# Units behind a norm done by halves of the tokens: the first gate unit of the two last FFNs and the first two units of the second gated-delta mixer

## The chip, the cores and the metric

The kernel runs on one core of a Trainium2 chip. The metric is the device time of one execution in microseconds. Three runs of the kernel before took 2135.91, 2136.45 and 2140.04 us, so the median is 2136.45 us.

## The reference

Six layers work on one sequence of 256 tokens with 1024 features, in float32. Layers 0 to 3 are post-norm: a mixer (gated delta net, HGRN2, GLA, gated delta net again), a layer norm over the scaled residual, a SwiGLU FFN of inner width 2816, and a layer norm again. Layers 4 and 5 are pre-norm: an RMS norm, a mixer of four parallel parts, the residual, an RMS norm, and an FFN whose inner activations go through a causal convolution of three taps before the gate.

```python
# layers 0 to 3
x = layer_norm(DN_ALPHA * x + m, mix_ln_g[i], mix_ln_b[i])
x = layer_norm(DN_ALPHA * x + swiglu(x, ffn_w_in[i], ffn_w_down[i]), ffn_ln_g[i], ffn_ln_b[i])
# layers 4 and 5, the FFN
h = rms_norm(x, ffn_norm_g[l])
u = causal_dwconv(jnp.einsum("bsd,df->bsf", h, ffn_w_in[l]), ffn_conv_w[l]) + ffn_conv_b[l]
gate, up = _split(u, (D_FF_2, D_FF_2))
x = x + jnp.einsum("bsf,fd->bsd", jax.nn.silu(gate) * up, ffn_w_out[l])
```

The mixer of layer 3 begins with a projection `x @ w_in` to 4112 columns: queries, keys and values (which go through a causal convolution of four taps), a gate, and 16 columns that hold beta and the decay of the eight heads.

## The kernel before

**Products.** A float32 product is done as three products of type fp32r. Weights and activations are each split into a high part (a cast to fp32r) and a low part (the rest): high times high, low weights times high activations, high weights times low activations. The activations of a stage stand in `xh` and `xl` as 8 tiles of 128 features by 256 tokens.

**Units.** Weights come in units of at most 128 x 2048 elements through a ring of six slots (SyncE starts the loads). ScalarE or VectorE casts a unit to its high part (`w_hi` or `w_extra`, L1624 and L2223), VectorE subtracts for the low part (`w_lo`, L2225; for some units GpSimd does three quarters, L1546). `pe_unit` is ticked when TensorE has done a unit, and that frees its slots.

**Two layouts of the result.** `token_products` (L586) has 128 tokens as the stationary operand and 512 channels as the moving one. `products` (L554) is channel-major: the weights are stationary, 128 channels at a time, and all 256 tokens are moving, so that the causal convolution runs along the free axis. A unit of 256 channels has two column tiles, 8 feature tiles and 3 products, so 48 matmuls, each with its own stationary operand. The first unit of the mixer in layer 3 (`pair8`) has only 40 columns and 24 matmuls.

**Behind a norm.** A norm is done by halves of 128 tokens (t = 0, 1), and each half by two chunks of 512 features (c = 0, 1). VectorE writes the normed rows (L2184), TensorE transposes them, four transposes to a chunk (`rows_to_channels`, L637, into a PSUM bank), ScalarE casts the bank to `xh` (`rows_high`), and VectorE subtracts for `xl` (`low_rows`). In `conv_ffn` (layers 4 and 5) and in `project` for the mixer of layer 3 TensorE does all sixteen transposes before the first matmul, and the matmuls with feature tile k wait for the chunk k // 4 of both halves (`all_rows`).

**Order of the work.** Every engine has its own queue, written out by hand, and runs it in order. In the RMS norm ahead of an FFN of layers 4 and 5 ScalarE does the squares of all four chunks of x first, then the four `rows_high`, then two casts of weights. In the layer norm ahead of layer 3's mixer VectorE does residual and statistics of half 0, its normed rows, residual and statistics of half 1, its normed rows, and then the four `low_rows` together (`all_at_once`); for the other layer norms the two `low_rows` of half 0 stand between the two chunks of half 1.

Of the kernel before, what the change touches and what calls it, by code (L numbers as in the profile page):

```python
# [29 lines left out]
P = 128  # L30
T = 256
D = 1024
KT = D // P
# [9 lines left out]
HALF = 128  # L43
ALL = slice(0, T)
# [173 lines left out]
def build(nc, A, out, book, layers=len(CHAIN)):  # L218

    book.restart()  # L220
    with ExitStack() as ctx:
# [31 lines left out]
        cols = sb("cols", [P, 4, 16])  # L253
# [40 lines left out]
        xh = over("xh", [P, KT, T], "inv")  # L294
        xl = over("xl", [P, KT, T], "xn")
# [226 lines left out]
        def _(pe):  # L522
            unit = fillers = 0

            def products(u, outs, tiles, width, moving, first=True, last=True, i=None, high_ready=None, low_ready=None,
                         part=range(10 ** 6)):


                n = tiles * width
                w_high = high_part(u)[:, 0:n].rearrange("p (k n) -> p k n", k=tiles)  # L530
                w_low = w_lo[:, u % RING, 0:n].rearrange("p (k n) -> p k n", k=tiles)
                x_high, x_low = moving
                if 0 in part:
                    pe.wait_ge(*hi_done(u, i))
                orders = [("high", w_high, x_high), ("w low", w_low, x_high), ("x low", w_high, x_low)]
                if not high_ready:
                    orders[1:] = orders[:0:-1]
                count = 0
                for step, (what, w, xin) in enumerate(orders):
                    if what == "w low" and count in part:  # L540
                        for low_part in lo_done(u, i):
                            pe.wait_ge(*low_part)
                    ready = high_ready if what == "high" else low_ready if what == "x low" else None
                    for j, (cols, c0, cw, tokens) in enumerate(outs):
                        for k in range(tiles):
                            count += 1
                            if count - 1 not in part:
                                continue
                            if ready and j == 0:
                                for what_ready in ready(k):  # L550
                                    pe.wait_ge(*what_ready)
                            wk, xk = w[:, k, c0:c0 + cw], xin[:, k, tokens]

                            m = nc.tensor.matmul(cols, *((wk, xk) if tokens == ALL else (xk, wk)),  # L554
                                                 start=(first and step == 0 and k == 0 and (j % 2 == 0)),
                                                 stop=(last and step == 2 and k == tiles - 1), skip_group_check=True)
                return m
# [93 lines left out]
            def project(layer, kind, norm):  # L651
                nonlocal unit
                psum.next = 4
                for n, (c0, w, how, name, idx) in enumerate(units_in(kind)):
                    if how == "tok0":
                        keys = ("unit", layer, n), ("unit", layer, n + 1)
                        if n == 0:
                            pair = [psum.claim(pe, "proj", layer, n, t) for t in range(2)]
                            second = [psum.claim(pe, "proj", layer, 2, t) for t in range(2)] if kind != "four" else [None]
                            pair_after_norm(unit, pair, norm, keys, second[0])  # L660
                        else:
                            token_pair(unit, second, keys)
                        unit += 2
                        continue
                    if how == "tok1":
                        continue
                    if late_gates(kind) and n >= len(units_in(kind)) - 2:
                        continue
                    ready = {}
                    if n == 0 and layer == 0:  # L670
                        pe.wait_ge(*pool_setup.at("gaps"))
                    if n == 0:
                        for t in range(2):
                            for c in range(2):
                                rows_to_channels(norm, t, c)
                        ready = all_rows(norm)
                    b = psum.claim(pe, "proj", layer, n)
                    left, right = b[:, 0:T], b[:, T:2 * T]
                    outs = {"cm": [(left, 0, P, ALL), (right, P, P, ALL)],
                            "pair8": [(b[0:40, 0:T], 0, 40, ALL)],  # L680
                            "row16": [(b[0:16, 0:T], 0, 16, ALL)],
                            "rest": [(b[0:100, 0:T], 0, 100, ALL)],

                            }[how]
                    products(unit, outs, KT, w, (xh, xl), **ready).then_inc(*pe_unit.tick("unit", layer, n))
                    unit += 1
                    if layer == 0 and n == 2:
                        params_to_columns()
                    if kind == "four":
                        four_ahead(layer, n)  # L690
                    if kind == "gla" and n == 6:
                        gla_gates(layer)
                    if kind == "gdn" and n == 4:
                        if layer == 0:
                            pe.wait_ge(*dve_setup.at("pick"))
                        gdn_columns(layer)
                    if kind == "gdn" and n >= N_CONV + 1:
                        qk_sums(layer, ((0, 1, 2), (3, 4, 5), (6, 7), ())[n - N_CONV - 1])
                    if kind == "gdn" and n == N_CONV + 3:
                        gdn_values(layer)  # L700
                        gdn_spread(layer, 0)
                        gdn_spread(layer, 1)

            def all_rows(norm):
                return {"high_ready": lambda k: (act_norm.at("x hi", norm, 0, k // 4), act_norm.at("x hi", norm, 1, k // 4)),
                        "low_ready": lambda k: (dve_norm.at("x lo", norm, 0, k // 4), dve_norm.at("x lo", norm, 1, k // 4))}
# [146 lines left out]
            def conv_ffn(layer, norm):  # L853

                nonlocal unit

                def gate_up(par_, key, i, freed, parts_ready={}):
                    nonlocal unit
                    for part in range(2):
                        b = banks[4 + 2 * par_ + part]  # L860
                        if freed is not None:
                            pe.wait_ge(*freed[part])
                        products(unit, [(b[:, 0:T], 0, P, ALL), (b[:, T:2 * T], P, P, ALL)], KT, T, (xh, xl), i=i,
                                 **(parts_ready if part == 0 else {}))\
                            .then_inc(*pe_unit.tick("gate" if part == 0 else "up", layer, key))
                        unit += 1

# [3 lines left out]
                def freed_by(k, ago=0):  # L871
                    return dve_ffn.at("conv gate", layer, k, ago=ago), dve_ffn.at("conv up", layer, k, ago=ago)

                for t in range(2):
                    for c in range(2):
                        rows_to_channels(norm, t, c, bank=2 * t + c)
                for b in range(4, 8):
                    psum.claim(pe, "ffn", layer, b, bank=b)
                gate_up(0, 0, None, None, all_rows(norm))
                gate_up(1, 1, None, None)  # L880
                for b in range(4):
                    psum.claim(pe, "ffn", layer, b, bank=b)
# [65 lines left out]
            def gdn_spread(layer, h):  # L948

                b = psum.claim(pe, "bcast", layer, h)  # L950
                for n, part in enumerate((rows_hi, rows_lo)):
                    m = nc.tensor.matmul(b[:, :], pick[0:8, h:h + 1].to_broadcast([8, P]),
                                         part[0:8, :, :].rearrange("p a n -> p (a n)"), start=(n == 0), stop=(n == 1))
                m.then_inc(*pe_gdn.tick("bcast", layer, h))
# [1215 lines left out]
        def _(dve):  # L2170
# [252 lines left out]
            def layer_norm(n, key, next_kind):  # L2423
# [21 lines left out]

                if key[0] == "out":
                    split(2)
                to_rms, all_at_once = next_kind == "four", next_kind == "gdn"
                chunk(0, 0)
                chunk(0, 1)  # L2450
                mean(0)
# [3 lines left out]
                if to_rms:  # L2455
                    dve.wait_ge(*gains_loaded(n + 1))
                    gained_rows(n + 1, 0)
                elif not all_at_once:
                    low_rows(n, 0, 0)
                    low_rows(n, 0, 1)  # L2460
                chunk(1, 1)
# [6 lines left out]
                normed(1, 1)  # L2468
                if to_rms:
                    gained_rows(n + 1, 1)  # L2470
                elif all_at_once:
                    low_rows(n, 0, 0)
                    low_rows(n, 0, 1)
                last = n + 1 if to_rms else n
                low_rows(last, 1, 0)
                low_rows(last, 1, 1)
# [488 lines left out]
```

## Time and profile before

| what | value |
|---|---|
| median of three runs | 2136.45 us |
| the profiled execution, its own time | 2137.8 us |
| its span | 2136.1 us |
| TensorE matmul busy | 2077.8 us, 97% |
| TensorE weight load busy | 1805.2 us, 85% |
| VectorE busy | 1488.5 us, 70% |
| ScalarE busy | 891.5 us, 42% |
| mean share of the granted TensorE clock | 0.993 |

PE is the matmul side of TensorE, PEld its weight loads, which run beside the matmuls. Both are pipelined: the duration of one matmul (283 ns with 256 moving columns) is longer than the distance from its start to the start of the next. So distances are read from a group's first start and the next group's first start, divided by the number of instructions, and not from the mean duration.

### The profile page before, as it was taken

The numbers are of one execution on the slowest core, as the hardware profiler recorded it, in microseconds if no ns is written. First come the engines' busy times: TensorE is split into PE (matmuls) and PEld (weight loads), VectorE is DVE, ScalarE is ACT, GpSimd is POOL, SyncE is SP. The second block draws the span as 40 slices with busy tenths as digits, with TensorE's granted clock in tenths as the row PEclk, the third lists the DMA queues.
The fourth block names the chain that finished last, engine by engine and source line by source line (L and its number), as shares of the span: only waits on it lengthen the run. The fifth ranks groups of instructions, "written<-read, shape, count | busy, mean of one in ns | idle before, by whom it ended". The sixth has DMA issues, their size and how long they took to land.

```text
span 2136.1 us, 35611 instructions
## 1 busy us (share of the span) xinstructions
PE 2077.8 (97%) x14377; PEld 1805.2 (85%) x14377; DVE 1488.5 (70%) x1941; ACT 891.5 (42%) x1174; POOL 177.8 (8%) x152
## 2 busy tenths in 40 slices
PE   7999999999999999999899999999989999999999
PEld 7988888798888798888798878887869998778998
DVE  5957754778854677744696685456688877588887
ACT  2254444334434423444323454445554334663332
POOL 5720000000000000000063300000100000100000
PEclk9999999999999999999999999999999999999999
DMA  7511655553555553555464046554325555414552
GB/s 227 178 61 61 205 189 191 170 190 99 180 196 182 173 178 119 197 192 182 139 180 155 3 149 216 186 186 154 103 78 171 186 183 170 138 50 158 194 180 99
DMA packets 267625, 333.81 MB, mean 156 GB/s; under 512 B 20562, under 2 KB 230613, under 8 KB 267493
## 3 DMA queue, kind: packets, MB, share of 16 engines
q1 hardware_dynamic: 267493, 331.93, 47.8%
q8 instruction: 98, 1.61, 0.3%
q14 instruction: 34, 0.28, 0.0%
HBM read 330.84 MB, written 1.05 MB: 155 GB/s over the span
## 4 chain that ended last, share of the span: by engine, by line
PE 86%; DVE 8%; ACT 3%; issue 2%; SPq 1%; DMA 0%; DVEq 0%; ACTq 0%
PE bank L586 45%; PE bank L554 29%; PE bank L1056 2%; DVE w_lo L2225 1%; ACT stat L1579 1%; PE bank L820 1%; PE bank L637 1%; DVE sq L2184 1%; PE bank L912 1%; PE bank L982 1%; PE bank L1137 1%; DVE pj L2184 1%; PE bank L926 1%; DVE xt L2184 1%; ACT w_hi L1624 1%
## 5 line engine op out<-in xcount | busy, mean ns | idle before, releaser
L2225 DVE TENSOR_TENSOR w_lo<-ring,w_hi 128x2048 fp32r<-128x2048 f32 (+2 forms) x289 | 615.2, 2131 | 375.3 <-ACT w_hi L1624 372.9
L1624 ACT ACTIVATE w_hi<-ring 128x2048 fp32r<-128x2048 f32 (+1 forms) x220 | 418.9, 1905 | 472.6 <-PE bank L586 287.3
L586 PE MATMUL bank<-w_lo,xh 128*128 128x512 f32 x992 | 267.7, 393 | 0.0
L554 PE MATMUL bank<-xh,w_hi 128*128 128x256 f32 x1752 | 239.9, 290 | 5.8 <-DVE w_hi L2223 5.0
L554 PE MATMUL bank<-xh,w_lo 128*128 128x256 f32 (+2 forms) x1832 | 242.4, 285 | 0.0
L586 PE MATMUL bank<-w_hi,xl 128*128 128x512 f32 x896 | 240.6, 390 | 1.0 <-DVE xl L2174 0.9
L586 PE MATMUL bank<-w_hi,xh 128*128 128x512 f32 x896 | 240.9, 391 | 0.6 <-ACT xh L1579 0.6
L554 PEld LDWEIGHTS bank<-xh,w_hi 128*128 128x128 f32 x1752 | 225.0, 195 | 15.8 <-issue 10.2
L554 PEld LDWEIGHTS bank<-xh,w_lo 128*128 128x128 f32 (+2 forms) x1832 | 229.1, 191 | 1.3
L554 PE MATMUL bank<-xl,w_hi 128*128 128x256 f32 x1752 | 230.1, 284 | 0.0
L554 PEld LDWEIGHTS bank<-xl,w_hi 128*128 128x128 f32 x1752 | 219.2, 192 | 0.4
L586 PEld LDWEIGHTS bank<-w_lo,xh 128*128 128x128 f32 x992 | 184.9, 188 | 37.9 <-DVE w_lo L2225 0.6
L586 PEld LDWEIGHTS bank<-w_hi,xh 128*128 128x128 f32 x896 | 167.1, 188 | 37.5 <-issue 2.0
L586 PEld LDWEIGHTS bank<-w_hi,xl 128*128 128x128 f32 x896 | 167.5, 188 | 36.9 <-DVE xl L2174 2.3
L1546 POOL TENSOR_TENSOR w_lo<-ring,w_hi 128x1536 fp32r<-128x1536 f32 x26 | 104.5, 4019 | 959.5 <-DVE w_hi L2223 959.5
L586 PE MATMUL bank<-w_hi,hid_hi 128*128 128x512 f32 x528 | 167.3, 398 | 2.0 <-DVE hid_lo L2174 2.0
L586 PE MATMUL bank<-w_hi,hid_lo 128*128 128x512 f32 x528 | 163.4, 391 | 0.0
L586 PE MATMUL bank<-w_lo,hid_hi 128*128 128x512 f32 x528 | 163.0, 390 | 0.0
L1579 ACT ACTIVATE yb<-bank 128x256 f32<-128x256 f32 (+4 forms) x146 | 58.9, 403 | 164.8 <-PE bank L586 124.9
L586 PEld LDWEIGHTS bank<-w_hi,hid_lo 128*128 128x128 f32 x528 | 99.1, 188 | 21.5
L586 PEld LDWEIGHTS bank<-w_lo,hid_hi 128*128 128x128 f32 x528 | 99.1, 188 | 21.5
L586 PEld LDWEIGHTS bank<-w_hi,hid_hi 128*128 128x128 f32 x528 | 94.6, 189 | 19.5 <-DVE hid_lo L2174 3.7
(323 smaller groups left out, 2406.0 us busy)
## 6 DMA issues: line engine op xcount, KB each, us to landing
ring<-in_ffn_w_in_dram SPq DMA_DIRECT2D x264, 512.0 KB, 4.4
ring<-in_ffn_w_down_dram SPq DMA_DIRECT2D x88, 512.0 KB, 4.1
ring<-in_gdn_w_in_dram SPq DMA_DIRECT2D x64, 512.0 KB, 5.0
ring<-in_ffn_w_out_dram SPq DMA_DIRECT2D x44, 512.0 KB, 3.9
ring<-in_w_in_dram SPq DMA_DIRECT2D x40, 512.0 KB, 4.7
ring<-in_hgrn_w_in_dram SPq DMA_DIRECT2D x32, 512.0 KB, 4.5
ring<-in_gla_w_in_dram SPq DMA_DIRECT2D x24, 512.0 KB, 4.6
ring<-in_gdn_w_out_dram SPq DMA_DIRECT2D x16, 512.0 KB, 4.5
```

The source lines that it names most:

```text
L554: m = nc.tensor.matmul(cols, *((wk, xk) if tokens == ALL else (xk, wk)), start=(first and step == 0 and k == 0 and (j % 2 == 0)), stop=(la ...
L586: m = nc.tensor.matmul(bank[:, 0:width], xin[:, k0 + k, rows_of], w[:, k, c * width:(c + 1) * width], start=(first and step == 0 and k == ...
L637: m = nc.tensor.transpose(b[:, j * P:(j + 1) * P], src[:, t, c * CHUNK + j * P:c * CHUNK + (j + 1) * P], ident[:, :])
L820: m = nc.tensor.transpose(banks[6][:, j * T + t * HALF:j * T + (t + 1) * HALF], hidt[:, t, j * P:(j + 1) * P], ident[:, :])
L912: nc.tensor.matmul(b[:, 0:T], k[:, 0:HALF], q[:, :], start=True, stop=True)
L926: nc.tensor.matmul(b[:, :], ones[:, :], gsq(g), start=True, stop=True).then_inc(*pe_gdn.tick("qk2", layer, g))
L1056: m = nc.tensor.matmul(b[r, c:c + HALF2], left[r, :], right[r, :], start=True, stop=True)
L1546: g.tensor_tensor(w_lo[:, unit % RING, part], ring[:, unit % RING, part], high_part(unit)[:, part], ALU.subtract).then_inc(*pool_lo.tick())
L1579: nc.scalar.activation(out_, in_, func, **kw).then_inc(*sig.tick(*key))
L1624: nc.scalar.activation(taken(high_part(u), u), taken(ring[:, u % RING, :], u), ACT.Copy).then_inc(*act_hi.tick())
L2184: v.scalar_tensor_tensor(out=out_, in0=a, scalar=s1, in1=b, op0=op0, op1=op1).then_inc(*sig.tick(*key))
L2225: v.tensor_tensor(w_lo[:, u % RING, 0:share], w[:, 0:share], high[:, 0:share], ALU.subtract).then_inc(*dve_lo.tick())
```

## The change

Three places are touched.

- `conv_ffn` (layers 4 and 5): the first gate unit is done by halves of the tokens. After the four-by-two transposes of half 0 come 32 matmuls of half 0 (high times high, low weights times high), then the transposes of half 1, the last 16 matmuls of half 0, and 48 matmuls of half 1.
- `project` for the mixer of layer 3: units 0 and 1 are done by halves in `first_units_by_halves`: transposes of half 0, the 24 matmuls of unit 0 and 32 of unit 1 for half 0, transposes of half 1, the remaining 16 of unit 1 for half 0, then 24 and 48 matmuls for half 1.
- The layer norm ahead of layer 3's mixer: the two `low_rows` of half 0 now stand between the two chunks of half 1, as in the other layer norms.

In each matmul of a half the weights stay stationary (128 x 128, or 128 x 40 in unit 0), and the moving operand has 128 tokens where it had 256.

```diff
@@ products @@
-                            m = nc.tensor.matmul(cols, *((wk, xk) if tokens == ALL else (xk, wk)),
+                            m = nc.tensor.matmul(cols, wk, xk,
@@ project @@
+                    if kind == "gdn" and layer and n < 2:
+                        if n == 0:
+                            first_units_by_halves(layer, norm)
+                        continue
+            def first_units_by_halves(layer, norm):
+
+                nonlocal unit
+                b0, b1 = psum.claim(pe, "proj", layer, 0), psum.claim(pe, "proj", layer, 1)
+
+                def narrow(t):
+                    of = slice(t * HALF, (t + 1) * HALF)
+                    return products(unit, [(b0[0:40, 0:T][:, of], 0, 40, of)], KT, 40, (xh, xl), first=(t == 0), **rows_of_half(norm, t))
+
+                def wide(t, part):
+                    of = slice(t * HALF, (t + 1) * HALF)
+                    return products(unit + 1, [(b1[:, 0:T][:, of], 0, P, of), (b1[:, T:2 * T][:, of], P, P, of)], KT, T, (xh, xl),
+                                    first=(t == 0), part=part)
+
+                for c in range(2):
+                    rows_to_channels(norm, 0, c)
+                narrow(0)
+                wide(0, range(0, 32))
+                for c in range(2):
+                    rows_to_channels(norm, 1, c)
+                wide(0, range(32, 48))
+                narrow(1).then_inc(*pe_unit.tick("unit", layer, 0))
+                wide(1, range(0, 48)).then_inc(*pe_unit.tick("unit", layer, 1))
+                unit += 2
+
+            def rows_of_half(norm, t):
+                return {"high_ready": lambda k: (act_norm.at("x hi", norm, t, k // 4),),
+                        "low_ready": lambda k: (dve_norm.at("x lo", norm, t, k // 4),)}
@@ conv_ffn @@
-                for t in range(2):
-                    for c in range(2):
-                        rows_to_channels(norm, t, c, bank=2 * t + c)
+                for c in range(2):
+                    rows_to_channels(norm, 0, c, bank=c)
                 for b in range(4, 8):
                     psum.claim(pe, "ffn", layer, b, bank=b)
-                gate_up(0, 0, None, None, all_rows(norm))
+
+                def first_gate(t, part, first):
+                    of = slice(t * HALF, (t + 1) * HALF)
+                    b = banks[4]
+                    return products(unit, [(b[:, 0:T][:, of], 0, P, of), (b[:, T:2 * T][:, of], P, P, of)], KT, T, (xh, xl), first=first,
+                                    part=part, **rows_of_half(norm, t))
+
+                first_gate(0, range(0, 32), True)
+                for c in range(2):
+                    rows_to_channels(norm, 1, c, bank=2 + c)
+                first_gate(0, range(32, 48), True)
+                first_gate(1, range(0, 48), False).then_inc(*pe_unit.tick("gate", layer, 0))
+                unit += 1
+                b = banks[5]
+                products(unit, [(b[:, 0:T], 0, P, ALL), (b[:, T:2 * T], P, P, ALL)], KT, T, (xh, xl)).then_inc(*pe_unit.tick("up", layer, 0))
+                unit += 1
                 gate_up(1, 1, None, None)
@@ layer_norm on VectorE @@
-                to_rms, all_at_once = next_kind == "four", next_kind == "gdn"
+                to_rms = next_kind == "four"
@@
-                elif not all_at_once:
+                else:
                     low_rows(n, 0, 0)
                     low_rows(n, 0, 1)
@@
-                elif all_at_once:
-                    low_rows(n, 0, 0)
-                    low_rows(n, 0, 1)
```

## Rows read from the trace of the kernel before

**Rows 1.** The page: busy us, share of the span, instructions; then the chain's shares.

```profile
PE 2077.8 (97%) x14377; PEld 1805.2 (85%) x14377; DVE 1488.5 (70%) x1941; ACT 891.5 (42%) x1174; POOL 177.8 (8%) x152
PE 86%; DVE 8%; ACT 3%; issue 2%; SPq 1%; DMA 0%; DVEq 0%; ACTq 0%
```

**Rows 2.** The chain of waits about layer 4's FFN norm: start, us, what.

```profile
1603.07 0.76 DVE sq L2184
...
1604.63 0.63 PE bank L637 x4
1605.26 0.11 issue
1605.38 7.67 PE bank L554 x50
```

**Rows 3.** The timeline there: start, us, engine, line, out<-in, count.

```profile
1602.94 1.07 ACT L1579 ACTIVATE xh<-bank 128x512 fp32r<-128x512 f32 x2
1603.97 1.29 PE L637 MATMUL bank<-ident,sq 128*128 128x128 f32 x8 [3.01 <-DVE sq L2184]
1605.38 3.60 PE L554 MATMUL bank<-xh,w_hi 128*128 128x256 f32 x16
1608.81 2.07 PE L554 MATMUL bank<-xh,w_lo 128*128 128x256 f32 x16
1610.72 2.08 PE L554 MATMUL bank<-xl,w_hi 128*128 128x256 f32 x16
1612.64 2.08 PE L554 MATMUL bank<-xh,w_extra 128*128 128x256 f32 x16
```

**Rows 4.** The timeline about layer 5's FFN norm.

```profile
1942.52 1.06 ACT L1579 ACTIVATE xh<-bank 128x512 fp32r<-128x512 f32 x2
1945.40 2.67 PE L554 MATMUL bank<-xh,w_hi 128*128 128x256 f32 x16
1951.75 2.08 PE L554 MATMUL bank<-xh,w_extra 128*128 128x256 f32 x16
```

**Rows 5.** The timeline about the norm ahead of layer 3's mixer.

```profile
1055.85 0.60 ACT L1579 ACTIVATE xh<-bank 128x512 fp32r<-128x512 f32 x1 [0.85 <-PE bank L637]
1056.28 0.67 DVE L2184 SCALAR_TENSOR_TENSOR xt<-xt,bank 128x512 f32<-128x512 f32 x1
1060.22 0.75 DVE L2184 SCALAR_TENSOR_TENSOR xt<-sq,moments,pj 128x512 f32<-128x512 f32 x1
1060.89 2.68 DVE L2174 TENSOR_TENSOR xl<-bank,xh 128x512 fp32r<-128x512 f32 x4
1061.79 0.83 PEld L554 LDWEIGHTS bank<-xh,w_extra 128*40 128x40 f32 x4
1072.42 2.08 PE L554 MATMUL bank<-xh,w_hi 128*128 128x256 f32 x16
```

**Rows 6.** Stretches: busy us (count) of each engine or of PE, then the granted clock's share.

```profile
1059.00:1066.00 7.00, 5.97 (x27) 4.83 (x28) 6.86 (x9) 1.20 (x2) 0.00 (x0) 0.51 0.00 1
1605.20:1608.70 3.50, 3.39 (x17) 0.51 0.00 0
```

**Rows 7.** Weight loads by form: count, busy us, mean ns of one, idle before.

```profile
L554 PEld LDWEIGHTS bank<-xh,w_lo 128*128 128x128 f32 x1792 | 223.4, 192 | 0.6
L554 PEld LDWEIGHTS bank<-xh,w_hi 128*100 128x100 f32 x16 | 2.0, 166 | 0.0
L554 PEld LDWEIGHTS bank<-xh,w_hi 128*16 128x16 f32 x8 | 0.8, 94 | 0.3
```

**Rows 8.** The timeline of five groups of loads and matmuls elsewhere.

```profile
1044.09 0.30 PEld L586 LDWEIGHTS bank<-w_hi,hid_hi 128*128 128x128 f32 x2
1089.79 0.32 PEld L934 LDWEIGHTS bank<-ident,rows 8*128 8x128 f32 x4
490.35 3.74 PE L1116 MATMUL bank<-pj,yb 128*128 128x128 f32 x32
490.24 3.66 PEld L1116 LDWEIGHTS bank<-pj,yb 128*128 128x128 f32 x32
1055.18 0.63 PE L637 MATMUL bank<-ident,xt 128*128 128x128 f32 x4 [0.82 <-DVE xt L2184]
```

**Rows 9.** The chain of waits, an undisturbed stretch of channel-major products.

```profile
1090.20 52.03 PE bank L554 x432
```

More of the change, by code:

```diff
@@ L855, in conv_ffn, with gate_up @@
                 nonlocal unit
-                def gate_up(par_, key, i, freed, parts_ready={}):
+                def gate_up(par_, key, i, freed):
                     nonlocal unit
@@ L862, in gate_up @@
                             pe.wait_ge(*freed[part])
-                        products(unit, [(b[:, 0:T], 0, P, ALL), (b[:, T:2 * T], P, P, ALL)], KT, T, (xh, xl), i=i,
-                                 **(parts_ready if part == 0 else {}))\
+                        products(unit, [(b[:, 0:T], 0, P, ALL), (b[:, T:2 * T], P, P, ALL)], KT, T, (xh, xl), i=i)\
                             .then_inc(*pe_unit.tick("gate" if part == 0 else "up", layer, key))
```

## The prediction

> **What bounds the kernel now.** The page comes first: matmuls are busy 97% of the span, weight loads 85%, and the chain that ends last runs over TensorE for 86% [rows 1]. The kernel is bound by TensorE's queue nearly everywhere, so what the change adds to it while nothing else is awaited goes into the time one for one, and it can gain only where TensorE waits. The chain of waits shows such a place: behind the norm ahead of layer 4's FFN it runs over VectorE's normed rows, four transposes and 0.11 us of issue into the products [rows 2]. The timeline gives the times: both casts of half 0 to xh are over at 1604.01 (the first of two, 0.60 us long, at 1603.54), while the first matmul starts at 1605.38 [rows 3]. Layer 5 has the same picture: first cast over at 1943.12, first matmul at 1945.40 [rows 4]. Ahead of layer 3's mixer the second cast of half 0 is over at 1056.45 and the first load of a product starts at 1061.79, a wait of over 5 us [rows 5]. The stretches show that behind these waits the granted clock is 0.51, the lower of its levels (1.2 GHz), for about 3.5 us in layer 4 and 7 us in layer 3 [rows 6]. So there are 1.8, 2.3 and 5.3 us in which work of half 0 could run, and some lost clock besides.
>
> **The price of half a matmul.** Everything hangs on one number: from start to start, how long takes a matmul with 128 x 128 fp32r weights and 128 moving tokens? With 256 tokens it is 52.03 us / 432 = 120 ns [rows 9]. The trace has no fp32r matmul with 128 moving columns; I bound it.
> - Lower end: half of 120 and the fixed part. 512 columns are not needed for that: 53 ns of columns at 2.4 GHz and the 13 ns by which 120 stands above 107 make 66 ns. It holds if the next load hides.
> - Upper end: the plain float32 matmuls of 128 x 128 x 128 at L1116 have two records each, 32 records in 3.66 us of loads, (3.66 - 0.19) / 31 = 112 ns apart, so 224 ns a matmul [rows 8]. It holds if fp32r with few columns falls back to float32's passes.
> - Between: the load. Every one of these matmuls needs other weights, so halving the tokens doubles the loads. A load's duration grows with its columns: 94 ns at 16, 166 at 100, 192 at 128, that is 98 / 112 = 0.87 ns a column, or 111 ns for 128 and about 80 ns of latency [rows 7]. Loads of fp32r weights that need not wait for matmuls show the same distance: two at 1044.09 take 0.30 us together, 0.30 - 0.19 = 0.11 us apart [rows 8]. That a load need not take so long is shown by the four small transposes, 0.32 us for four loads of 128 columns, 61 ns apart, but those load plain rows for a transpose, not fp32r weights [rows 8].
>
> I take 114 ns: the load's own 107 to 112 ns and a few more. The row nearest to the case (same weights, same type) is the pair of loads at 0.11 us. So half a matmul costs nearly what a whole one does, and a unit done by halves costs nearly twice as much.
>
> Here a page of the Trainium skill speaks too. "TensorE: Matmul & The Clock Gate", section "LDWEIGHTS (loading the stationary operand)", gives columns / 1.2 ns for a load, 107 ns for 128; by that rule, with which the 0.11 us of [rows 8] agrees, the sum is the one below. The same page's section "Back-to-back issue gap" says that in a stream of pairs the measured distance at 128 columns is about 81 ns; no row here shows a distance under 107 for such weights. By an estimate from that 81 the three places would give about -0.4, 0 and -2.4 us, so 2133.6 us in all, hardly a change.
>
> **The change part by part.**
> 1. *Layer 4, first gate unit.* Removed: 48 matmuls, 1605.38 to 1612.64 (7.26 us; the first 16 take 3.43 instead of 1.92 us at the lower clock) [rows 3]. Added: 96 matmuls, 96 x 114 = 10.9 us. The start moves to 1603.6, when the first cast of half 0 is over. The eight transposes of half 1 were ahead of the products and are now within: (0.63 - 0.27) / 3 = 0.12 us apart [rows 8], 0.9 us. ScalarE's casts of half 1 follow 0.9 us behind each chunk, and 16 matmuls of half 0 (1.8 us) cover them. End: 1603.6 + 10.9 + 0.9 = 1615.4, against 1612.64: **+2.8 us** at the full clock. With 66 ns: 1610.8, -1.9. With 224: 1603.6 + 21.5 + 0.9 = 1626.0, +13.4.
> 2. *Layer 5, the same.* 1943.2 + 11.8 = 1955.0 against 1951.75 [rows 4]: **+3.3 us**. With 66: 1950.4, -1.4. With 224: 1965.6, +13.8.
> 3. *Layer 3, low_rows moved.* Two of VectorE's four, 2.68 / 4 = 0.67 us each [rows 5], now stand before the last chunk of half 1 on VectorE's queue. Everything queued behind them, the statistics, normed rows and with them the transposes of half 1, comes 1.34 us later: the last normed rows end at 1060.97 + 1.34 = 1062.3. TensorE waits for it.
> 4. *Layer 3, units 0 and 1.* Half 0 of unit 0 is 24 matmuls with 40 stationary columns; a load of 40 columns is short (16 take 94 ns, near the latency alone [rows 7]), so 66 ns each, done when the second low_rows is, at 1057.7, plus four matmuls: 1058.0. Then 32 x 114 = 3.7: 1061.7. Transposes: the second chunk waits until 1062.45, over at 1062.9. Then 16 x 114 = 1.8 (1064.7), 24 x 66 = 1.6 (1066.3) and 48 x 114 = 5.5: 1071.8, against 1072.42 [rows 5]: **-0.6 us**, although 7 us at the lower clock go. With 66 everywhere: 1058.0 + 2.1, a wait to 1062.9, then 1.1 + 1.6 + 3.2 = 1068.8, -3.6. With 224 (also for unit 0): 5.3 + 7.2 + 0.9 + 3.6 + 5.3 + 10.8 from 1055.05 on make 1088.2, +15.8.
> 5. *The clock.* The terms above are at the full clock. A stretch like that of layer 4 (3.5 us at 0.51) costs 1.7 us if it falls on loads. In layers 4 and 5 the idle time ahead of the first matmul shortens by only 2 us, so I expect it to stay in part; in layer 3 TensorE is busy most of the time from 1055 on. None costs 0, all three 5.1; I take **+2.0**, a little over one stretch.
> 6. *Costed at nothing.* In layers 4 and 5 ScalarE's two casts of weights behind `rows_high` start 3.5 us later; they and VectorE's low parts are for the third and fourth unit, which TensorE starts 6 us after the second. No DMA is added; the loads of the ring wait for a unit's end and move with it. Without that cover a low part late by 2.3 us would be added once. The matmuls behind are bound by TensorE [rows 9], so nothing takes the delay back.
>
> Sum: 2.8 + 3.3 - 0.6 + 2.0 = **+7.5 us**. The profiled execution took 2137.8 us (span 2136.1), so it would be 2145.3; it lies 1.35 us above the median of the runs shown, and for the median the sum gives 2136.45 + 7.5 = **2143.9 us**. Its own range, with 112 to 120 ns and none to three lower-clock stretches, is 2140 to 2149.
>
> **The rivals.**
> - *The load hides* (faster). The point from which it decides is 120 ns / 2: if a load of 128 fp32r columns occupies TensorE for under about 66 ns, half matmuls cost half. Then -1.9, -1.4 and -3.6 make -6.9, with a stretch or two at the lower clock -4: 2129.5 to 2132.5. For it: the four loads 61 ns apart. Against it: 0.87 ns a column and the pair at 0.11 us.
> - *fp32r falls to float32's passes* (much slower). +13.4 + 13.8 + 15.8 = +43: 2179 us. For it: nowhere in the trace has an fp32r matmul under 256 moving columns, so nothing excludes it. Against it: 256 and 512 columns cost the same per column, with no sign of another mode.
> - *No change to speak of.* The matmuls cost 114 ns or somewhat less and the clock stays up in all three places; the wait gained in layer 3 pays more than reckoned: 2137 to 2140.
>
> **How the numbers follow.** A measurement of this kernel tells about 0.2% (4.3 us) from no change, so "same" is 2132.2 to 2140.7. Chances: forecast 0.70 (of it 0.05 under 2140.7), load hidden 0.10 (0.09 of it faster), float32's passes 0.12, no change 0.08. That gives faster 0.09, same 0.14, slower 0.77. The range 2132 to 2151 holds the forecast, the third rival and the edge of the first, and leaves the 2179 out.
>
> **What would show it.** In the changed profile: loads of `xh,w_hi` with 128x128 and matmuls with 128x128 about 114 ns apart, in three places (66 or 224 for the rivals); the second unit of layer 4's FFN starting some 2.8 to 4.5 us later after the same norm; VectorE's last normed rows of layer 3 1.3 us later; the clock at 1.00 from 1055 to 1072. Wrong would be the forecast if the 96 matmuls of a gate took under 9 or over 13 us, or if the delay behind a gate were made up before the first down unit.

## The result, and the profile after

The changed kernel took 2157.43 us (median of four runs, 2156.54 to 2164.90), the kernel before 2136.94 us beside it (2135.91 to 2140.04). By the medians that is 20.5 us slower, where +7.5 us and at most 2151 us were forecast. The ratio is 1.0105, 95% interval 1.009 to 1.012, which is 22 us (19 to 26). The two measures differ a little here and below; a difference given behind a ratio is worked out from that ratio. The profiled execution of the changed kernel is its longest, 2164.9 us (span 2163.2); against the profiled one of before that is 27.1 us.

The timeline of the changed kernel about layer 4's FFN answers to [rows 3], about layer 5's to [rows 4], and about the mixer of layer 3 to [rows 5]. Columns as there: start, us, engine, line, out<-in, count.

```profile
1604.70 1.29 PE L637 MATMUL bank<-ident,sq 128*128 128x128 f32 x8 [0.29 <-DVE sq L2230]
1608.70 3.64 PE L554 MATMUL bank<-xh,w_hi 128*128 128x128 f32 x16 [2.71 <-ACT xh L1625]
1612.14 3.62 PE L554 MATMUL bank<-xh,w_lo 128*128 128x128 f32 x16
1615.56 1.93 PE L637 MATMUL bank<-ident,sq 128*128 128x128 f32 x8
1617.14 2.75 PE L554 MATMUL bank<-xl,w_hi 128*128 128x128 f32 x16
1619.72 1.95 PE L554 MATMUL bank<-xh,w_hi 128*128 128x128 f32 x16
1621.51 1.95 PE L554 MATMUL bank<-xh,w_lo 128*128 128x128 f32 x16
1625.09 2.12 PE L554 MATMUL bank<-xh,w_extra 128*128 128x256 f32 x16
...
1951.94 1.29 PE L637 MATMUL bank<-ident,sq 128*128 128x128 f32 x8 [0.30 <-DVE sq L2230]
1955.94 2.98 PE L554 MATMUL bank<-xh,w_hi 128*128 128x128 f32 x16 [2.71 <-ACT xh L1625]
1973.99 3.62 PE L554 MATMUL bank<-xl,w_hi 128*128 128x128 f32 x16
1977.40 3.53 PE L554 MATMUL bank<-xh,w_extra 128*128 128x256 f32 x16
1980.77 2.08 PE L554 MATMUL bank<-xl,w_extra 128*128 128x256 f32 x16
```

```profile
1053.17 0.63 PE L637 MATMUL bank<-ident,xt 128*128 128x128 f32 x4 [0.85 <-DVE xt L2230]
1055.72 1.27 DVE L2220 TENSOR_TENSOR xl<-bank,xh 128x512 fp32r<-128x512 f32 x2
1058.09 3.62 PE L554 MATMUL bank<-xh,w_hi 128*128 128x128 f32 x16
1060.83 0.75 DVE L2230 SCALAR_TENSOR_TENSOR xt<-sq,moments,pj 128x512 f32<-128x512 f32 x1
1064.92 1.93 PE L637 MATMUL bank<-ident,xt 128*128 128x128 f32 x8
1074.36 1.95 PE L554 MATMUL bank<-xl,w_hi 128*128 128x128 f32 x16
1077.93 2.13 PE L554 MATMUL bank<-xh,w_hi 128*128 128x256 f32 x16
```

Sixteen half matmuls (matmuls with 128 moving tokens) take 1619.72 to 1621.51, 1.79 us or 112 ns each, in one part of the trace, and 1608.70 to 1612.14, 3.44 us or 215 ns each, in another. The first is the price I took (114 ns). The second is not 224 ns of another mode but the same matmul at half the clock, as the stretches show (busy us with count, then the granted clock's share, for layer 4 with the busy time of PE, PEld, DVE, ACT and POOL in this order; the last two numbers of a line are DMA's). Layer 3 and layer 5:

```profile
1055.60:1072.40 16.80, 16.46 (x99) 0.50 0.10 34
1072.70:1078.00 5.30, 5.30 (x50) 1.00 0.63 198
...
1956.80:1977.40 20.60, 20.60 (x98) 0.50 0.00 1
1977.40:1980.50 3.10, 3.10 (x16) 0.50 0.57 164
1980.70:1985.00 4.30, 4.30 (x38) 1.00 0.32 112
```

Layer 4:

```profile
1608.60:1618.70 10.10, 10.00 (x48) 10.03 (x48) 3.36 (x6) 2.22 (x4) 0.00 (x0) 0.50 0.02 7
1618.90:1625.00 6.10, 6.10 (x57) 6.10 (x56) 4.49 (x2) 2.82 (x2) 0.00 (x0) 1.00 0.00 0
```

Before, 7 us at 0.51 followed the norm of layer 3 and about 3.5 us that of layer 4 [rows 6]. Now it is 17, 10 and 24 us, with TensorE busy all but 0.3, 0.1 and 0 us of it. In layer 5 the clock is at its lower level (1.2 GHz) through the whole unit by halves and comes back only in the next unit, whose matmuls have 256 columns; in layers 3 and 4 it comes back within the units by halves, at 1072.6 and 1618.8.

The places can be laid side by side from their first transpose of half 0 to the first matmul of the next whole unit. Layer 4 went from 1599.67 to 1612.64, 12.97 us, before, and takes 1604.70 to 1625.09, 20.39 us, after. The other entries are made in the same way from each kernel's profile:

| profiled run of | layer 3 | layer 4 | layer 5 |
|---|---|---|---|
| before | 18.69 us | 12.97 us | 12.51 us |
| changed | 24.71 | 20.39 | 25.46, and 1.4 in the next unit |
| mixer alone (e1) | 17.55 | | |
| twice the columns (e4) | 19.40 | 17.91 | 17.97 |
| changed, with filler (e7) | 17.55 | 15.60 | 15.60 |
| before, with filler (e6) | 16.93 | 11.76 | 11.74 |

The changed kernel's row is 6.0 + 7.4 + 12.9 + 1.4 = 27.7 us over the one of before, which is the difference of the spans (27.1 us) within a microsecond. So between these two profiled runs the rest of the kernel adds under a microsecond. That is not so in every pair: for e4 the places add up to 11.1 us and the spans differ by 8.4, for e7 4.6 and 1.3, since stretches at the lower clock elsewhere vary from run to run.

### The profile page after: what moved, and what is told of

Read it like the earlier page. It is cut to its first block, busy times and chain, and to the rows that moved or that the text cites. A ratio compares the mean times of both kernels' runs of the same rounds, so it can differ in the third digit from the quotient of the medians.

```text
span 2163.2 us, 35904 instructions
## 1 busy us (share of the span) xinstructions
PE 2111.1 (98%) x14545; PEld 1840.3 (85%) x14545; DVE 1487.9 (69%) x1941; ACT 891.7 (41%) x1174; POOL 177.8 (8%) x152
## 4 chain that ended last, share of the span: by engine, by line
PE 87%; DVE 7%; ACT 3%; issue 2%; SPq 1%; DMA 0%; DVEq 0%; ACTq 0%
PE bank L586 44%; PE bank L554 30%; PE bank L1102 2%; DVE w_lo L2271 1%; ACT stat L1625 1%; PE bank L637 1%; PE bank L853 1%; PE bank L958 1%; PE bank L1028 1%; PE bank L1183 1%; DVE sq L2230 1%; DVE pj L2230 1%; PE bank L972 1%; ACT w_hi L1670 1%; PE bank L963 1%
## 5 line engine op out<-in xcount | busy, mean ns | idle before, releaser
L554 PE MATMUL bank<-xh,w_hi 128*128 128x256 f32 (+3 forms) x1800 | 249.1, 293 | 9.6 <-ACT xh L1625 5.4
L554 PE MATMUL bank<-xh,w_lo 128*128 128x256 f32 (+3 forms) x1888 | 254.9, 289 | 0.0
L554 PEld LDWEIGHTS bank<-xh,w_hi 128*128 128x128 f32 (+2 forms) x1800 | 233.9, 198 | 19.6 <-issue 14.8
L554 PEld LDWEIGHTS bank<-xh,w_lo 128*128 128x128 f32 (+2 forms) x1888 | 241.4, 196 | 1.2 <-issue 0.2
L554 PE MATMUL bank<-xl,w_hi 128*128 128x256 f32 (+3 forms) x1800 | 241.7, 288 | 0.0
L554 PEld LDWEIGHTS bank<-xl,w_hi 128*128 128x128 f32 (+2 forms) x1800 | 230.6, 197 | 0.4
```

What stands on the lines that cost most here:

```text
L554: m = nc.tensor.matmul(cols, wk, xk, start=(first and step == 0 and k == 0 and (j % 2 == 0)), stop=(last and step == 2 and k == tiles - 1) ...
```

## The experiments

Two theories stood at first. By W, half matmuls keep the granted clock at its lower level. By I, the clock falls by the wait alone and half matmuls have no part in it. H is what the first four runs (e1, e2, e4, e5) left: the wait lowers the clock, and half matmuls keep the level that they find.

**e1: only the mixer of layer 3.** The FFNs are those of the kernel before.

```diff
...
+                for t in range(2):
+                    for c in range(2):
+                        rows_to_channels(norm, t, c, bank=2 * t + c)
...
+                gate_up(0, 0, None, None, all_rows(norm))
...
```

> Only the mixer of layer 3 (units 0 and 1 by halves, low_rows moved), both FFNs as before. The changed kernel's trace gives this place 6.0 us. Theory W (matmuls with 128 moving columns keep the granted clock at its lower level): +6 us, about 2143, with the clock at 0.50 from the first products of half 0 until the first product with 256 columns. Theory I (the clock falls by the wait alone and the half matmuls have no part in it): the clock is low for some 3 to 7 us as before, and the place costs -1 to +2 us.

Measured: 2134.86 us (ten runs, 2133.20 to 2141.66), ratio 1.0001 (0.9991 to 1.0012). Neither theory as put, though the time (+0.2 us by the ratio) lies in theory I's -1 to +2 us: the profiled run has the clock at 1.00 throughout the place, and the place takes 1.1 us less than before, where the prediction had -0.6.

```profile
1053.00:1070.80 17.80, 15.99 (x160) 15.33 (x160) 16.77 (x20) 6.73 (x10) 3.52 (x1) 1.00 0.47 147
```

```profile
1054.78 0.63 PE L637 MATMUL bank<-ident,xt 128*128 128x128 f32 x4 [0.82 <-DVE xt L2217]
1059.25 1.95 PE L554 MATMUL bank<-xl,w_hi 128*128 128x128 f32 x16
1061.04 0.62 PE L637 MATMUL bank<-ident,xt 128*128 128x128 f32 x4
1064.08 0.65 PE L554 MATMUL bank<-xh,w_extra 128*40 128x128 f32 x8
1064.56 0.64 PE L554 MATMUL bank<-xh,w_lo 128*40 128x128 f32 x8
```

Three of its ten runs took 2138.2 to 2141.7 us with a mean granted clock of 0.992 to 0.994, the other seven 2133.2 to 2135.9 with 0.994 to 0.996. These times alone don't show that the mixer is the cause, for the kernel before ran beside it from 2132.7 to 2139.1 us. The profiles do: the same instructions take 17.55 us here with the clock up and 24.71 us in the changed kernel, where it fell at 1055.6. TensorE stood still for the same short times about that point in both (0.85, 0.82 and 0.45 us, with transposes and four matmuls between), so what makes the clock fall in one run and not in the other is open. The last two lines also settle what makes the 112 ns: eight matmuls with 128 moving columns and only 40 stationary ones are (1064.56 - 1064.08) / 8 = 60 ns apart. The columns that stream are the same; what is gone is the load of the other 88.

**e2: only the FFNs of layers 4 and 5.**

```diff
-                    if kind == "gdn" and layer and n < 2:
+                    if False:
...
+                elif all_at_once:
+                    low_rows(n, 0, 0)
+                    low_rows(n, 0, 1)
```

> Only the first gate unit of the FFNs of layers 4 and 5 by halves, mixer as before. Theory W: 96 matmuls at 213 to 220 ns where the clock stays low; together +14 to +21 us, 2151 to 2158, and from run to run it differs by how many half matmuls run at the lower clock. Theory I: only the load term, +6 us (2.8 and 3.3), 2143.

Measured: 2156.39 us (2150.64 to 2158.84), ratio 1.0091 (1.0075 to 1.0108), as W had it. The long stretch is in layer 4 this time, with the same instructions:

```profile
1604.40:1626.00 21.60, 21.60 (x104) 0.50 0.00 1
1626.10:1628.20 2.10, 2.10 (x11) 0.50 0.32 79
1628.40:1633.00 4.60, 4.60 (x41) 1.00 0.51 179
1959.50:1966.10 6.60, 6.60 (x34) 0.50 0.00 0
1966.40:1972.00 5.60, 5.60 (x53) 1.00 0.01 3
```

In layer 5 the clock rose at 1966.2, within half matmuls, 1.3 us behind the eight transposes of half 1. The same happened in layer 4 of the changed kernel (transposes until 1617.1, rise at 1618.8). So a rise within the unit is possible, and whether it comes differs by place and run. I, with 2143 us, is out.

**e4: each half's tokens streamed twice.** Same order, same loads, double the columns.

```diff
+                            if tokens != ALL and cw == P:
+                                xk = xin[:, k, tokens].rearrange("p (a n) -> p a n", a=1).to_broadcast([P, 2, HALF])
                             m = nc.tensor.matmul(cols, wk, xk,
...
-                    return products(unit, [(b[:, 0:T][:, of], 0, P, of), (b[:, T:2 * T][:, of], P, P, of)], KT, T, (xh, xl), first=first,
+                    return products(unit, [(b[:, 0:T], 0, P, of), (b[:, T:2 * T], P, P, of)], KT, T, (xh, xl), first=first,
...
```

> The changed kernel, but each 128x128 matmul of a half has its 128 tokens twice as moving operand (256 columns, both column halves of the bank), so that the number of loads and the order stay and only the columns double; the sums of the two token halves are mixed by it. Theory W: the clock comes back soon as behind the norms of before, and although every matmul has twice the columns the kernel is faster than the changed one: 4.5 to 7 us over the kernel before instead of 20 (96 x 120 ns for 96 x 114 ns). Theory I: the clock stays low as long as in the changed kernel, and the time is the same or up to 2 us longer: +20 to +23.

Measured: 2146.07 us (2144.68 to 2147.80), ratio 1.0052 (1.0036 to 1.0069), +11 us. TensorE streams twice the columns in these units and the kernel is 11 us faster than the changed one. The mean granted clock of its four runs is 0.994 to 0.995, that of the changed kernel's four 0.984 to 0.989. After the wait the clock is low for the first matmuls and then comes back:

```profile
1601.59 3.61 PE L556 MATMUL bank<-xh,w_hi 128*128 128x256 f32 x16 [2.71 <-ACT xh L1627]
1605.03 2.08 PE L556 MATMUL bank<-xh,w_lo 128*128 128x256 f32 x16
1606.95 1.03 PE L639 MATMUL bank<-ident,sq 128*128 128x128 f32 x8
1607.74 2.16 PE L556 MATMUL bank<-xl,w_hi 128*128 128x256 f32 x16
```

My number for it was too low (4.5 to 7): it left out one such low start in each FFN, 3.44 us where 16 matmuls take 1.92 at the full clock. The places in the table give 0.7 + 4.9 + 5.5 = 11.1. Theory I, +20 to +23, is out.

**e5: units by halves in a full queue.** The kernel before; the gate and up units of the FFNs' second step are done by halves, with no wait anywhere near.

```diff
...
-                gate_up(1, 1, None, None)
+                for part in range(2):
+                    b = banks[6 + part]
+                    for t in range(2):
+                        of = slice(t * HALF, (t + 1) * HALF)
+                        m = products(unit, [(b[:, 0:T][:, of], 0, P, of), (b[:, T:2 * T][:, of], P, P, of)], KT, T, (xh, xl),
+                                     first=(t == 0))
+                    m.then_inc(*pe_unit.tick("gate" if part == 0 else "up", layer, 1))
+                    unit += 1
```

> The kernel before, but the gate and up units of the second step of the FFNs of layers 4 and 5 are done by halves (4 x 96 matmuls with 128 columns in place of 4 x 48 with 256), where all inputs are there and TensorE never waits. Theory W: the granted clock falls to 0.50 although there is no wait ahead, and stays there until matmuls with more columns follow; more than the load term, +30 to +60 us. Theory I: the clock stays 1.00; 4 x (96 x 112 - 48 x 120 ns) = +20 us, 2156.

Measured: 2157.07 us (2153.91 to 2157.55), ratio 1.0099 (1.0082 to 1.0116), +21 us. Here I is right and W wrong: the clock stays at 1.00 over 21 us of half matmuls in both layers, and the 21 us are the loads alone (4 x (96 x 112 - 48 x 120) ns = 20 us).

```profile
1618.10:1639.40 21.30, 21.30 (x194) 1.00 0.37 124
1966.50:1987.50 21.00, 21.00 (x191) 1.00 0.30 101
```

So half matmuls do not pull the clock down, and with e2 and e4 they do not readily bring it back. That is theory H; the two rises within half matmuls in e2 and in the changed kernel show that it holds mostly, and not always.

**e3: the two low_rows moved, nothing else.**

```diff
-                elif not all_at_once:
+                else:
                     low_rows(n, 0, 0)
                     low_rows(n, 0, 1)
...
-                elif all_at_once:
-                    low_rows(n, 0, 0)
-                    low_rows(n, 0, 1)
```

> Only part 3 of the change: in the layer norm ahead of layer 3's mixer the two low_rows of half 0 stand between the chunks of half 1; all products as before. The prediction's step: everything behind comes 1.34 us later and TensorE waits for it, +1.3 us. Rival: the two low_rows are taken out of a stretch behind the last normed rows that TensorE waits for as well, so the sum stays within 1 us of the kernel before. In the trace VectorE's last normed rows must end 1.3 us later after TensorE's last matmul of the FFN.

Measured: 2137.93 us (2135.59 to 2140.33), ratio 1.0006 (0.9996 to 1.0016). The time doesn't tell 1.3 us from none. The trace shows the step: from the first statistics of half 1 to the end of the last normed rows it is 1055.56 to 1062.03, against 1055.67 to 1060.97 before, 1.17 us more. TensorE does wait for it: its first product starts 9.29 us behind its first transpose (1062.91 to 1053.62), against 8.13 us before. Yet the whole place takes 18.57 us against 18.69, for in this run the clock came back sooner: the 24 matmuls with 40 stationary columns took 3.54 us in place of 4.80. The rival's reason doesn't hold: before, the low parts were ready at 1063.57 and first used at 1065.54, so nothing waited for them.

**e6: fillers in the kernel before.** The kernel has a helper, `stay_awake(n, bank)`, that issues n plain float32 matmuls whose results are not used. It is placed in the three waits.

```diff
                             for c in range(2):
                                 rows_to_channels(norm, t, c)
+                            if t == 0 and layer:
+                                stay_awake(9, 7)
...
                         rows_to_channels(norm, t, c, bank=2 * t + c)
+                    if t == 0:
+                        stay_awake(6, 4)
```

> The kernel before with float32 filler matmuls of 256 columns (idle work, results unused) in the three waits: 9 behind half 0's transposes ahead of layer 3's mixer, 6 behind those of each FFN of layers 4 and 5. Theory H (half-wide matmuls hold the clock at full level but do not lift it; it is the wait that lowers it): the clock stays 1.00 in the three places and the lower-clock cost of before goes: -3.4 -1.5 -0.6, about 2130.5. If fillers do not hold the clock: 2136 to 2137, no change.

Measured: 2134.64 us (2132.97 to 2136.72), ratio 0.9987 (0.9977 to 0.9996), -2.8 us (0.9 to 4.9). The medians differ by 2.0 us. The clock stays up in the three places, and the ten runs have a mean granted clock of 0.995 to 0.997, against 0.991 to 0.994 in all 31 runs of the kernel before beside them. So it was the wait without matmuls that cost the clock. The gain is half of the 5.5 us expected. The profile's places give 1.76 + 1.21 + 0.77 = 3.7 us. In the mixer it is 1.76 and not 3.4, since in a part of that stretch TensorE waits for VectorE and ScalarE at either clock (0.36 and 0.34 us before, 0.82 and 0.31 us here).

```profile
1052.90:1069.80 16.90, 14.91 (x106) 1.00 0.47 148
1596.00:1607.00 11.00, 10.05 (x65) 1.00 0.47 169
```

**e7: fillers in the changed kernel.**

```diff
                 for c in range(2):
+                    stay_awake(2, 7)
                     rows_to_channels(norm, 0, c)
                 narrow(0)
...
                     rows_to_channels(norm, 0, c, bank=c)
+                stay_awake(5, 4)
```

> The changed kernel with filler matmuls in its waits: 2 ahead of each chunk of half 0's transposes in the mixer, 5 behind half 0's transposes in each FFN. Theory H: the clock is never low when the half-wide matmuls start, they run at 112 ns each, and only the load term is left: +2.8 +3.3 -1 = +5 us, about 2141. Theory W as first put (half-wide matmuls lower the clock by themselves): still +13 to +21 us, since each place begins with half-wide matmuls anyway.

Measured: 2140.50 us (2139.16 to 2143.90), ratio 1.0019 (1.0009 to 1.0029), +4 us. With the clock up in all three places, the changed kernel's order costs what its loads cost:

```profile
1052.70:1070.20 17.50, 16.78 (x164) 1.00 0.46 145
1596.40:1612.00 15.60, 15.00 (x122) 1.00 0.27 93
1937.40:1953.00 15.60, 15.01 (x123) 1.00 0.26 88
```

Some 16 of the changed kernel's 20.5 us are gone by adding work to TensorE's queue.

e6 and e7 together are the fair comparison of the two orders, with the clock up in both. By halves every place is slower: 17.55 us against 16.93 in the mixer, 15.60 against 11.76 and 11.74 in the FFNs. The medians are 2140.50 and 2134.64 us, 5.9 us apart. So starting half 0 in the wait never paid for its loads; the 1.1 us that the mixer won in e1 were the lower clock of before.

**e8: mixer by halves, FFNs whole, fillers in all three waits.**

The edit is that of e7 in the mixer and that of e6 in the FFNs.

> The mixer of layer 3 by halves as changed, the FFNs whole as before, filler in all three waits. Theory H: the mixer never falls into the lower clock (no runs at +6 us as with the mixer alone), -3 to -5 us there against before, and -2 us in the FFNs: 2130 to 2132, and all runs within 2 us of each other in place of 8.5. Without an effect of the filler: as the mixer alone, 2133 to 2142.

Measured: 2134.40 us (2132.83 to 2136.84), ratio 0.9990 (0.9980 to 1.0000), not told apart from e6. The ten runs lie within 4.0 us, those of e1 within 8.5 (2 us were expected), and the profile's mixer takes 17.55 us as in e1 and e7; the 0.6 us by which that is over e6 are too small for the medians. The time missed the 2130 to 2132 us expected.

**e9: e6 and a fourth wait, ahead of layer 4's mixer.**

```diff
...
+                            if layer == DEPTH:
+                                stay_awake(8, 7)
                             pair = [psum.claim(pe, "proj", layer, n, t) for t in range(2)]
...
```

> The kernel before with the fillers of e6 and 8 more in the wait ahead of layer 4's mixer (TensorE stands still for 3.8 us there, and 6.8 us at the lower clock follow). Theory H: that stretch goes or shrinks to half, -1.5 to -3 us against e6, 2131.5 to 2133, faster than both kernels. If the transposes of half 0 are held up by the filler: as e6 or up to 1 us slower.

Measured: 2133.74 us (2131.83 to 2135.96), ratio 0.9987 (0.9977 to 0.9996). It is faster than both kernels, but the fourth filler's own share can't be told from e6, which has the same ratio. In its profile the expected 1.5 to 3 us don't come either. The filler holds the clock at 1.00 through its wait and until 1459, but behind a later wait of 1.87 us the clock is low all the same, 0.61 in 1459.5 to 1463.5. From TensorE's last matmuls of layer 3 to the first matmul of L554 it is 22.0 us, against 21.8 in e6: in this profile the stretch at the lower clock stands at another point and is not gone.

**e10: a filler between the halves, at the low clock.** The changed kernel; eight fillers behind half 1's transposes in each FFN, so that half matmuls stand on both sides of them.

```diff
                     rows_to_channels(norm, 1, c, bank=2 + c)
+                for _ in range(8):
+                    nc.tensor.matmul(banks[7][:, 0:T], ones[:, :], strict[:, 0:T], start=True, stop=True)
```

> The changed kernel with 8 filler matmuls of 256 columns (idle work) in each FFN between the transposes of half 1 and the products that follow, at a point where the clock is low. Theory H (128 moving columns cannot lift the clock, 256 can): the clock comes back to 1.00 within or right behind the filler, and the 48 matmuls of half 1 run 112 ns apart in every profile; the filler costs 3.4 to 6 us in each FFN and saves up to 5, so the time is within 5 us of the changed kernel's 2157. If the clock came back by the time since the wait alone, the low stretches would be as long as in the changed kernel (10 and 24 us).

Measured: 2158.46 us (2157.44 to 2159.13), ratio 1.0104 (1.0087 to 1.0121), as the changed kernel. In the stretches of layers 4 and 5 the clock is low up to and into the fillers (which begin at 1611.07 and 1961.09) and at 1.00 behind them:

```profile
1605.50:1611.00 5.50, 5.50 (x28) 0.50 0.02 3
1611.10:1612.30 1.20, 1.20 (x4) 0.50 0.00 0
1612.40:1622.20 9.80, 9.80 (x78) 1.00 0.00 0
1953.80:1961.10 7.30, 7.30 (x37) 0.50 0.01 2
1961.10:1963.90 2.80, 2.80 (x8) 0.50 0.00 0
1964.00:1973.00 9.00, 9.00 (x74) 1.00 0.00 0
```

The 64 half matmuls behind them that ran 215 ns apart in layer 5 of the changed kernel run 112 ns apart here (the first 16 of them 120). What they save, the fillers cost (3.9 us in layer 4, 4.7 in layer 5). The mean granted clock of the four runs is 0.991 to 0.993, against 0.984 to 0.989 in the changed kernel and 0.987 to 0.990 in e2, so there was less of the lower clock in every run.

That it was the fillers that lifted the clock is not shown for each place. The low stretches here are 6.8 and 10.2 us long, and stretches of 6.8 us (layer 5 of e2) and 10.2 us (layer 4 of the changed kernel) ended with no filler there; in layer 4 the rise comes 1.2 us behind the transposes, as in e2. Those two rises also contradict theory H as this expectation words it. The fillers differ from half matmuls in more than their width, too; the run that changes the width alone is e4.

## Why the prediction was wrong

- *The price of half a matmul* was right. 114 ns were taken; 112 ns were measured at the full clock, in the changed kernel, e5 and e7. The row that carried it was the pair of loads 0.11 us apart [rows 8], and e1's matmuls with 40 stationary columns show that it is the load. The rival in which the load hides (66 ns) and the one with float32's passes (224 ns) are out, and so is the estimate at 81 ns: at the full clock no group of 16 half matmuls in the profiles was under 111.
- *Parts 1 and 2* (+2.8 and +3.3 at the full clock) were right: +2.6 and +3.1 in e7. They are small because the kernel before pays for a low start there; against e6, with the clock up, a unit by halves costs 3.8 and 3.9 us.
- *Parts 3 and 4* were right: -0.6 forecast, -1.1 in e1 and e7 (against e6 it is +0.6); VectorE's last normed rows came later, 1.2 us in e3 for 1.34.
- *Part 5, the clock, is the step that failed.* I took +2.0 and set the bounds at 0 and 5.1 us, "all three" stretches of 1.7 us each, though [rows 6] had 7 us at 0.51 in layer 3. In the profiled run the clock's part is 27.1 - 4.6 = 22.5 us (4.6 us being e7's three places over those of before), in the medians 20.5 - 4.1 = 16.4 us (4.1 us being e7's difference). I had priced the lower clock as a stretch of fixed length that a wait leaves behind, read off from [rows 6], where it was followed by matmuls of 256 columns. I did not ask whether the new instructions behind the wait would end it as the old ones did. They don't, mostly, and doubling their columns took 11 us off again (e4). A unit of 96 loads at the lower clock takes about 20 us in place of 11, so the bound should have been the length of the new work (some 10 us a unit: 96 x (215 - 112) ns), not the length of the old stretch. The forecast's own sign of being wrong, over 13 us for the 96 matmuls of a gate, is there: 14.8 us in layer 4 and 19.9 in layer 5 of the profiled run, the transposes between taken off. "In layer 3 TensorE is busy most of the time from 1055 on", the reason for the clock staying up there, was right in the profile of e1 and wrong in the changed kernel's profile.
- *Part 6*, edits costed at nothing, held: the three places make up the difference of the profiled runs within a microsecond.
- The sign was right, and the reason given for it too, but the larger part of the loss came from a term taken as a small correction. Where a term is a state with two levels, its bound is all the work that can run at the lower one.

## What to carry to other kernels

Before splitting a matmul's moving side, compare the load's own distance with the time of the moving columns: with fp32r weights of 128 columns and 128 tokens it is 112 ns, with 40 stationary columns and the same tokens 60 ns (e1). So here half the tokens cost 93% of the whole (112 of 120 ns). And look at what stands first behind a wait: units by halves mostly kept the clock at the level they found, 1.00 in a full queue and 0.50 behind a wait. Matmuls of no use in the wait made both orders faster, -2.8 us (0.9 to 4.9) for the kernel before and some 16 us for the changed one. For filling such a wait they were the better work, since they leave the number of loads in the units behind as it was: e6 is 5.9 us under e7 with the clock up in both.

## What the runs showed of the hardware that I had not expected

- A queue that is busy without a gap can stay at 1.2 GHz for 24 us (layer 5 of the changed kernel, 20.6 us of half matmuls at 0.50 and 3.1 us of the next unit), while the same kind of half matmuls runs 21.3 us at 1.00 when it finds the clock so (e5).
- Doubling the streamed columns of a stretch made the kernel 11 us faster (e4 against the changed kernel).
- The clock sometimes rose within a unit by halves: 1.3 and 1.7 us behind eight transposes (layer 5 of e2, layer 4 of the changed kernel), and in layer 3 of the changed kernel at 1072.6, behind 24 matmuls with 40 stationary columns. In layer 5 of the changed kernel and layer 4 of e2, with the same eight transposes in it, the same unit went on at 0.50 to its end. What decides between these stays open; no run was made for it.
